# Row sums by four 64x64 tiles, a smaller DMA scratch, more key-value chunks kept, fewer row buffers

## What is computed

```python
def peer_ffn(h, w_q, sub_keys, u_tab, v_tab):
    q = (xt @ w_q).reshape(T, 8, 2, 128)
    s = jnp.einsum('thpd,hpnd->thpn', q, sub_keys)
    # ... best 16 of 128 x 128 pairs for each of 8 heads -> eidx, gates: (T, 128)
    uc, vc = jnp.take(u_tab, ic, axis=0), jnp.take(v_tab, ic, axis=0)
    act = jax.nn.gelu(jnp.einsum('cd,ckd->ck', xc, uc))
    return jnp.einsum('ck,ckd->cd', gc * act, vc)
```

## Time and profile before

| | |
|---|---|
| median of the runs | 2730.17 us |
| span of the profiled execution | 2730.7 us |
| PE matmul busy | 2497.4 us, 91% |
| PE weight loads busy | 1284.3 us, 47% |
| DVE busy | 1372.8 us, 50% |
| ACT busy | 626.5 us, 23% |
| POOL busy | 494.7 us, 18% |
| read from HBM | 1055.64 MB, 388 GB/s over the span |
| rows by POOL's queue | 540.07 MB |
| weights by SP's queue | 516.70 MB |

### The profile page before, as it was taken

The page is one execution under the profiler, slowest core; times in us unless marked ns, Lnnn a source line. Parts: engine busy times, 40 slices in busy tenths (PEclk is TensorE's granted clock), DMA queues, the critical chain, the costliest instruction groups (busy, mean ns, idle before and its releaser), DMA issues.

```text
span 2730.7 us, 30447 instructions
## 1 busy us (share of the span) xinstructions
PE 2497.4 (91%) x10712; PEld 1284.3 (47%) x10712; DVE 1372.8 (50%) x3805; ACT 626.5 (23%) x1464; POOL 494.7 (18%) x534
## 2 busy tenths in 40 slices
PE   8899999999999999997987889989799899788786
PEld 6744444444444444995643334436344446333332
DVE  2411222222212222757677776785675775678753
ACT  0300110100100001232322342332332432332212
POOL 1000000000000000003333333332332332333330
PEclk9989999999999999998999999999999999999999
DMA  7689999999999997549999999999999999999993
GB/s 250 262 325 409 429 428 429 428 428 428 428 429 427 430 427 296 183 170 381 421 420 421 421 419 383 419 420 418 420 418 417 420 418 417 417 411 421 421 421 165
DMA packets 135686, 1058.03 MB, mean 387 GB/s; under 512 B 15744, under 2 KB 16168, under 8 KB 45472
## 3 DMA queue, kind: packets, MB, share of 16 engines
q0 software_dynamic: 75104, 540.07, 47.9%
q1 hardware_dynamic: 60480, 516.70, 45.8%
HBM read 1055.64 MB, written 2.63 MB: 388 GB/s over the span
## 4 chain that ended last, share of the span: by engine, by line
PE 55%; DMA 28%; DVE 12%; ACT 3%; issue 2%; SPq 0%; DVEq 0%; POOL 0%; POOLq 0%
PE ps L773 15%; PE ps L1245 15%; DMA big<-in_uv,small 14%; DMA big<-in_w_gate_up 13%; PE ps L763 4%; PE ps L927 4%; DVE big L2170 4%; PE ps L1042 2%; PE ps L1198 2%; PE ps L1058 2%; PE ps L809 1%; PE ps L623 1%; PE ps L695 1%; DMA ring<-in_uv,small 1%; PE ps L1005 1%
## 5 line engine op out<-in xcount | busy, mean ns | idle before, releaser
L1245 PE MATMUL ps<-big,small 128*128 128x512 f32 x1940 | 922.5, 622 | 171.1 <-ACT small L1669 170.9
L2342 POOL DMA_INDIRECT big<-in_uv,small x485 | 458.9, 946 | 2086.6 <-DVE small L2150 1182.7
L773 PE MATMUL ps<-big 128*64 128x512 f32 x3072 | 701.7, 601 | 11.6 <-DMA big<-in_w_gate_up 7.7
L2170 DVE SCALAR_TENSOR_TENSOR big<-big,ps 128x1024 f32<-128x1024 f32 x485 | 580.8, 1217 | 213.9 <-DMA big<-in_uv,small 213.6
L1245 PEld LDWEIGHTS ps<-big,small 128*128 128x128 f32 x1940 | 371.7, 199 | 662.1 <-issue 410.7
L773 PEld LDWEIGHTS ps<-big 128*64 128x64 f32 x3072 | 205.5, 137 | 397.7 <-issue 355.4
L1669 ACT ACTIVATE small<-con,small 128x128 f32<-128x128 f32 x512 | 177.6, 394 | 322.4 <-DVE small L2199 273.2
L1908 DVE COPY big<-ps 128x512 f32<-128x512 f32 x32 | 22.1, 692 | 417.5 <-PE ps L773 417.5
L1894 DVE TENSOR_TENSOR big<-ps,big 128x256 f32<-128x256 f32 x64 | 27.2, 425 | 284.7 <-PE ps L791 284.7
L1664 ACT ACTIVATE small<-small 128x2 f32<-128x2 f32 x224 | 45.7, 204 | 495.1 <-DVE big L2170 479.1
L927 PEld LDWEIGHTS ps<-hT,ring 128*128 128x128 f32 x1152 | 134.5, 194 | 14.7 <-issue 10.5
(11 more groups left out here) (338 smaller groups left out, 2104.8 us busy)
## 6 DMA issues: line engine op xcount, KB each, us to landing
big<-in_w_gate_up SPq DMA_DIRECT2D x128, 2048.0 KB, 21.0
big<-in_w_down SPq DMA_DIRECT2D x64, 2048.0 KB, 22.4
ring<-in_peer_w_q SPq DMA_DIRECT2D x48, 512.0 KB, 10.7
ring<-in_ple_w_gate SPq DMA_DIRECT2D x22, 512.0 KB, 10.5
ring<-in_w_kv SPq DMA_DIRECT2D x22, 512.0 KB, 10.4
ring<-in_w_in SPq DMA_DIRECT2D x16, 512.0 KB, 7.1
ring<-in_a_w_in SPq DMA_DIRECT2D x16, 512.0 KB, 4.7
ring<-in_b_w_q SPq DMA_DIRECT2D x16, 512.0 KB, 11.7
```

The source lines that it names most:

```text
L773: last = pe.matmul(ps[side * CAP:(side + 1) * CAP, bank + b, :], o, w[:, at:at + BANK], start=start, stop=stop, skip_group_check=True)
L1245: last = pe.matmul(ps[:, out_bank(f) + z, :], diagonal(k), rows(k)[:, D + z * BANK:D + (z + 1) * BANK], start=(k % PHASE == 0), stop=((k + ...
L2170: ins = dve.scalar_tensor_tensor(r, r, 1.0, tok, op0=ALU.mult, op1=ALU.mult, accum_out=dots[:, k % PICKS:k % PICKS + 1])
L2342: pool.indirect_dma_start(out=rows(k), out_offset=None, in_=io[f"uv{n // UNITS}"], in_offset=bass.IndirectOffsetOnAxis(ap=rows_at[:, at:at ...
```

## The change

- A pick is four matmuls instead of two. The diagonal is kept folded, as 128 partitions x 64 columns (partition p has its coefficient at column p mod 64). Tokens 0 to 63 and 64 to 127 are multiplied apart, each for two halves of the columns, on the four 64x64 quadrants of the array. Tokens 0 to 63 get their first 512 columns in partitions 0 to 63 of the first bank and the other 512 in partitions 64 to 127 of it; tokens 64 to 127 likewise in the second bank.
- `merge` puts this right: ACT and DVE copy one half of a bank each to `gatebuf` (`keep_sums`), and PE writes them to the other half with two matmuls by the identity. It stands at the ADD step of the chain, and for the last phase at tick 56; the picks of the last eight ticks write each token's columns to their final place (`by_halves`), on two quadrants.
- The scratch for dynamic DMA falls from its default of 16 KB to 4 KB per partition, and a new buffer `spare` takes the 12 KB.
- EARLY is 13 instead of 10, and the first seven chunks (three in `spare`, four in the space of two former row buffers) stay for the second token tile, which loads only nine.
- Row buffers: 10, and one more (ring slots) from pick 170 on, instead of three.

```diff
-ROWS, MORE_ROWS, MORE_AT = 10, 3, 170
+ROWS, MORE_ROWS, MORE_AT = 10, 1, 170
...
-EARLY = 10
+EARLY, RESIDENT = 13, 7
+AHEAD = (EARLY, RESIDENT)
+SCRATCH = 4096
...
-        early = [at(k * D, D) for k in (0, 1, 2, 3, 6, 7, 8, 9, 10, 11)]
+        early = [tile(spare, k, D) for k in range(3)] + [at(k * D, D) for k in (8, 9, 10, 11, 0, 1, 2, 3, 6, 7)]
...
                     pe.wait_ge(S["diags_ready"], k + 1)
-                    for z in range(2):
-                        last = pe.matmul(ps[:, out_bank(f) + z, :], diagonal(k),
-                                         rows(k)[:, D + z * BANK:D + (z + 1) * BANK],
-                                         start=(k % PHASE == 0), stop=((k + 1) % PHASE == 0), skip_group_check=True)
+                    by_halves = f == LAST and t >= LAST_MERGE
+                    for r, tokens_ in enumerate(sides_of_rows()):
+                        for z, at in enumerate(sides_of_rows()):
+                            bank = out_bank(f) + (z if by_halves else r)
+                            last = pe.matmul(ps[tokens_ if by_halves else at, bank, :], diagonal(k)[tokens_, :],
+                                             rows(k)[tokens_, D + z * BANK:D + (z + 1) * BANK],
+                                             start=(k % PHASE == 0), stop=((k + 1) % PHASE == 0), skip_group_check=True)
                     last.then_inc(S["rows_used"], 1)
+
+            def merge(f):
+
+                low, high = sides_of_rows()
+                pe.wait_ge(S["sums_kept"], 2 * f + 2)
+                pe.matmul(ps[low, out_bank(f) + 1, :], ident[high, high], gatebuf[high, 0:BANK], start=True, stop=True,
+                          skip_group_check=True)
+                pe.matmul(ps[high, out_bank(f), :], ident[low, low], gatebuf[low, 0:BANK], start=True, stop=True,
+                          skip_group_check=True).then_inc(S["tile_done"], 1)
...
+                if t == ADD:
+                    merge(q)
...
+                    if f == LAST and t == LAST_MERGE:
+                        merge(f)
+                        pe.wait_ge(S["tile_done"], merged(f))
                     picks(f, t)
...
+            def keep_sums(f):
+
+                low = sides_of_rows()[0]
+                act.wait_ge(S["rows_used"], PHASE * f + (2 * LAST_MERGE if f == LAST else PHASE))
+                act.copy(gatebuf[low, 0:BANK], ps[low, out_bank(f) + 1, :]).then_inc(S["sums_kept"], 1)
...
-                    act.activation(diagonal(k), ident, ACT.Copy, scale=coef[:, k % PICKS:k % PICKS + 1])\
+                    act.activation(diagonal(k), fold, ACT.Copy, scale=coef[:, k % PICKS:k % PICKS + 1])\
...
                 if t == ADD:
                     dve.wait_ge(S["x_kept"], 2 * tt + 2)
+                    if q < LAST:
+                        keep_sums(q)
+                    dve.wait_ge(S["tile_done"], merged(q))
                     dve.wait_ge(S["rows_used"], PHASE * (q + 1))
                     add(out_bank(q))
...
-    nc = bacc.Bacc("TRN2", target_bir_lowering=False, num_devices=1)
+    nc = bacc.Bacc("TRN2", target_bir_lowering=False, num_devices=1, dynamic_dma_scratch_size=SCRATCH)
```

More of the change, by code:

```diff
@@ L72 @@
 DIAGS = 8
+SIDE = P // 2
+LAST_MERGE = 56
 BIG = 16 * ROW
@@ L88 @@
 LAST, LAST_PROJ = PHASES - 1, 40
+MERGED_BEFORE = 7
 FIRST_NEXT, ASK_HERE, ASK_NEXT = 0, 11, 19
@@ L234, in program @@
         pT = sb("pT", [P, 2 * T])
+        spare = sb("spare", [P, 3 * D])
         ps = ctx.enter_context(nc.psum_tensor("ps", [P, 8, BANK], F32))
@@ L390, in program @@
         dots, acts, coef = (small[:, 1536 + k * PICKS:1536 + (k + 1) * PICKS] for k in range(3))
-        diag_at = small[:, 2304:2304 + DIAGS * P]
+        diag_at = small[:, 2304:2304 + DIAGS * SIDE]
+        fold = small[:, 2816:2816 + SIDE]
         def rows(n):
@@ L397, in rows, with sides_of_rows, merged @@
                 return big[:, b * ROW:(b + 1) * ROW]
-            if b < ROWS + 2:
-                return at(10 * D - (b - ROWS) * ROW, ROW)
             return ring[:, CHAIN_RING:RING, :].rearrange("p k d -> p (k d)")
         def diagonal(n):
-            return diag_at[:, n % DIAGS * P:(n % DIAGS + 1) * P]
+            return diag_at[:, n % DIAGS * SIDE:(n % DIAGS + 1) * SIDE]
+        def sides_of_rows():
+            return slice(0, SIDE), slice(SIDE, P)
+        def merged(f):
+            return MERGED_BEFORE + f + 1
         def tok_bank(f):
@@ L572, in _ @@
                 ple_chain(q)
-                for k in range(EARLY if q == 0 else 0, 2 * DT):
+                for k in range(AHEAD[q], 2 * DT):
                     c, z = k % DT, k // DT
-                    load(first[f"kv{q}"] + k - (EARLY if q == 0 else 0),
+                    load(first[f"kv{q}"] + k - AHEAD[q],
                          io["w_kv"][c * P:(c + 1) * P, z * SLOT:(z + 1) * SLOT])
@@ L1049, in key_value @@
                         k = z * DT + c
-                        if q:
-                            w = chunk(first[f"kv{q}"] + k)
-                        elif k < EARLY:
+                        if k < AHEAD[q]:
                             pe.wait_ge(early_loaded, 16 * EARLY)
@@ L1055, in key_value @@
                         else:
-                            w = chunk(first["kv0"] + k - EARLY)
+                            w = chunk(first[f"kv{q}"] + k - AHEAD[q])
                         for half_ in range(2):
@@ L1060, in key_value @@
                                              start=(c == 0), stop=(c == DT - 1), skip_group_check=True)
-                        last.then_inc(w_used if q or k >= EARLY else S["early_used"], 1)
+                        last.then_inc(w_used if k >= AHEAD[q] else S["early_used"], 1)
                 def turned(src, bank):
@@ L1537, in gain @@
                                            scale=col(name, at + c)).then_inc(S["hd_act"], 1)
+                if t == ADD and q < LAST:
+                    keep_sums(q)
                 if t == SQUARE and q < LAST:
@@ L1699, in _ @@
                                 .then_inc(S["x_kept"], 1)
+                    if f == LAST and t == LAST_MERGE:
+                        keep_sums(f)
                     if f:
@@ L1992, in _ @@
             ins.then_inc(S["sums_in"], 1)
+            dve.tensor_tensor(fold, ident[:, 0:SIDE], ident[:, SIDE:P], ALU.add)
             lam = par[:, PARAMS["lam"][0]:PARAMS["lam"][0] + DT]
@@ L2295, in chain, with keep_sums @@
                     gain(2, B, (hd, "norm_ffn", DT))
+            def keep_sums(f):
+                high = sides_of_rows()[1]
+                dve.wait_ge(S["rows_used"], PHASE * f + (2 * LAST_MERGE if f == LAST else PHASE))
+                dve.tensor_copy(gatebuf[high, 0:BANK], ps[high, out_bank(f), :]).then_inc(S["sums_kept"], 1)
             for piece in range(4):
```

13 lines of the change are left out of this document (6 added, 7 removed).

## The result

The changed kernel takes 2719.16 us (median of 6 runs, 2715.12 to 2723.59), the kernel before 2731.61 us in the same series (median of 6, 2728.17 to 2738.91): a ratio of 0.9945, 95% interval 0.9932 to 0.9958, 12.5 us less. The forecast was 2717 us. The profiled execution of the changed kernel took 2715.61 us with a span of 2713.5 us, which is 17.2 us less than the profiled one of before. I put 4 us of these to the scatter of the first half and not to the change.

The account below looks back on a forecast made before the run. The lagging one of 16 DMA engines was taken to bound the second half. Terms -12.9 + 0.7 - 1.0 + 0 = -13.2 us took the 2730.7 us span to 2717.5, median 2717 us; range 2709 to 2733.

Parts of the forecast that it names:

- The bound: Second half, row transfers: the one DMA engine that lags sets the pace, 2.485 us per row, 1.29 per chunk.
- Fewer bytes: Chunk loads of the second half: the lagging engine sheds ten at 1.29 us each, -12.9 us; three moved loads free.
- Four tiles: Picks on PE: four quadrants at once, 1.0 us per pick (bounds 0.86 and 1.72), tick 5.4 to 5.6 us.
- What PE gives back: Stretches where PE held up transfers: the lagging engine recovers 0 to 8 us, taken as -1.0 us.
- PE's fetches: Instruction fetches on queue 8: 16 more of 16 KB, spread over the DMA engines, +0.7 us.
- That rival (2731): PE's added instruction fetches load the lagging DMA engine and give back 10 to 16 us: no change; chance 0.13.
- Merges, buffers, scratch, tail: Four merges, eleven row buffers and 4 KB scratch cost 0; the time after the last row stays 31.5 us.
- Two tiles at a time only: Picks on PE overlap only two ways, 1.72 us each: about 6 us more, 2723 us; chance 0.10.
- The clock: PE, less busy, gets a lower clock in ticks with chunks: +37 us, 2754 us, slower; chance 0.11.
- All that PE lost comes back: Stretches where PE held up transfers: the lagging engine recovers 8 us instead of 1, 2710 us; chance 0.06.

Follow-up runs that it names:

- the tiles alone: The changed kernel with the loads of the kernel before (10 chunks early, none kept for the second token tile): median 2733.78 us, ratio 0.9996 to the kernel before.

## Why the prediction was right

The time came within 2.2 us of the forecast (2719.16 against 2717), and the row phase fell by 13.3 us where the sum had 13.2. That these agree to 0.1 us is luck: a single profile tells 2 us, and the small terms of the sum, +0.7 and -1.0, are below that. The large one, the bytes, carries the result. By its own steps:

- *The bound.* Right. Two runs speak for it: the tiles alone cure the dip of the mean (388 to 419 GB/s) and gain nothing, and 16 more fetches of queue 14, 0.13 MB in all, cost 17.8 us. That the work of one engine is the bound is inferred from these, from the 25 GB/s at the end and from the steps; no trace names the engine. The whole sum is a weaker support than it looks. Rows and chunks, 1272 and 121 x 1.29 = 156 us, are 1428 of 1453.5 us and leave 25.5; before, 1441 of 1466.8 leave 26. But queue 14 has 38 fetches in each, not the twenty that the prediction took. At 0.95 us each they are 36 us, more than what is left, and the start must fit in it too: the first dot product begins 11.4 us after the first issue. A part is counted twice, as the 90 us from which a chunk's 1.29 us were read the earlier trace rows hold two such fetches, here of before at 2040 to 2130 us:

  ```profile
  q14 instruction: 2, 0.02, 0.0%
  ```

  Without them a chunk is 1.21 us. What else is too large isn't known. The differences between runs were tested, and the whole sum was not.
- *Fewer bytes, -12.9.* Right in size where PE can follow: -13.4 between tiles only and after. Without the tiles it was -10.3. The three moved loads were free: nothing moves from 1202 to 1215 us (1 GB/s), and PE starts on peer_w_q without a wait, as before.
- *Four tiles.* 0.94 us per pick, taken 1.0, bounds 0.86 and 1.72. The tick is 5.51 us, forecast 5.4 to 5.6. The two changes of tile shape in it cost 0.2 us, as taken: the chunk block takes 3.63 us (1654.73 to 1658.36), 3.43 before. A full drain at each change, as the Trainium skill has it (TensorEngine Tiling (Array Packing), Key Properties), was priced at twice 0.43 us; the chunk block shows a quarter of that. The pick block, 1.88 us, is itself 0.16 us over the 1.72 of four tiles at once, so the two changes cost 0.4 us at most.
- *What PE gives back, -1.0.* None of it shows: tiles alone +0.1, which holds the fetches, the merges, the buffers and the scratch as well; no run takes them apart. In the change as a whole the tiles seem to be worth 3 us, but as the cover of the bytes' gain, which the sum held as a condition and not as a term.
- *PE's fetches, +0.7.* 16 more on queue 8 and as many as before on queue 14 (38), as worked out, and no cost that can be seen; 33 more on top cost nothing in the row phase either. That rival (2731) is out.
- *Merges, buffers, scratch, tail.* Nothing together: the tiles-only kernel has the merges, eleven buffers and the small scratch, and its row phase is that of before. Scratch and buffers cost nothing by runs of their own as well; the merges have none, and a loss there that PE's give-back makes good would not be seen. The tail is 31.5 us. The last eight ticks work by halves: 32 records in 8.88 us right behind the merge, then 16 in 3.70 us at 2664.40 us, as forecast, and in time for the rows. Eight buffers would have cost 7 us, so the margin that I read from the landing times ends between ten and eight.
- *Two tiles at a time only.* It didn't happen, but the run with the old picks, which take as long, gives its price: 3.0 us, not 6. What covered the other half is not shown.
- *The clock.* It fell where I had said it might and did no harm. Granted 0.80 to 0.86 in most stretches and 0.76 at 2500 to 2550 us; in chunk ticks the blocks of 16 passes take 1.95 us, at 2.4 GHz. At the lower level, 1.2 GHz, are many picks between waits, 3.69 us of a 4.97 us tick. The Trainium skill, TensorE: Matmul & The Clock Gate, What's actually happening, has the clock follow how busy the engine was lately and halve when it idles. The trace agrees that the lower level comes behind waits, 2.02 us in the block at 2638.61 us, but not behind each; a pick block of after at the higher level behind a longer one:

  ```profile
  1769.02 1.95 PE L1262 MATMUL ps<-big,small 64*64 64x512 f32 x16 [3.28 <-ACT small L1706]
  ```

  What the rival priced didn't happen. It had slow ticks with chunks, of 7.55 us and 74% busy, at the lower level. The chunk matmuls of the phase (L1055, L1069, L1095) take 0.59 us in the median and none over 0.92. Where I looked (1596 to 1622 and 2049 to 2077 us), such ticks stand in runs, 5.5 to 6.4 us each, with waits of under 1 us, and the long wait comes behind the run (5.22 us at 1622 us), where only picks are slow.
- *All that PE lost comes back* (2710): out, by the tiles alone.

What I hadn't foreseen is the scatter of the first half, which is as large as the effect: the first row is issued between 1228.48 and 1240.67 us.

## What to carry to other kernels

When the slowest of the 16 DMA engines sets the pace, count its work in transfers and fetches; a dip in the mean GB/s can then be no loss, and its cure no gain. Remove bytes first, and then give the compute engine the room to follow them: here the second part gained nothing by itself, and likely 3 us with the first. To see effects of 0.1 to 0.5%, compare the phase that the change touches, from its first to its last event, and not the whole span.

## What the runs showed of the hardware

- Four 64x64 tiles of fp32 matmuls of 512 columns run at once: 16 passes in 1.88 us, where eight passes of 128x128 take 3.43 us; on two tiles at a time 16 passes take 3.70 us.
- A fetch of 8 KB on queue 14 (128 DVE instructions: 2048 added, 16 fetches more) makes a row phase bound by transfers 1.1 us longer, and a row beside it lands 0.95 us late; fetches of 16 KB on queue 8 cost the row phase nothing, up to 79 of them.
- A chunk of 0.5 MB loaded by two DMAs in place of one, in between row gathers, makes the phase 2.1 to 2.3 us longer, in 64 + 64 partitions as in 120 + 8; the DMA share stays full and 398 to 400 GB/s pass in place of 417 (1720 to 2150 us).
- A dynamic-DMA scratch of 4 KB serves thirteen buffers of 1 MB, nine to ten rows in flight at a time, without a loss (1467.6 against 1466.8 us).
